# Head norm of the RWKV output moved from the output stage into the scan

## Chip, cores and metric

The kernel runs on one core of one Trainium2 chip. The metric is the device time of one execution in microseconds. Engines are named PE (matrix engine), DVE (vector), ACT (scalar), POOL (GpSimd) and SP (issues DMAs).

## What is computed

Two layers of a trunk over 2,048 tokens of width 1,024, all in float32. Each layer normalises x, projects it with one matrix of 3,972 columns, runs four mixers side by side (forgetting attention, RWKV-7, windowed attention, a short convolution), gates each with silu, projects back and adds x. The part that matters is the end of the RWKV-7 mixer, where y comes from a scan over tokens with 4 heads of 64 channels:

```python
mean = jnp.mean(y, axis=-1, keepdims=True)
var = jnp.mean((y - mean) ** 2, axis=-1, keepdims=True)
y = ((y - mean) * lax.rsqrt(var + RWKV_LN_EPS)).reshape(B, S, GROUP_W)
y = y * ln_g.astype(f32) + ln_b.astype(f32)
bonus = jnp.sum(r_h * k_h * r_k.astype(f32), axis=-1, keepdims=True) * v_h
y = y + bonus.reshape(B, S, GROUP_W)
```

## The kernel before

A layer is a series of stages with a barrier between them: `phase_project` (norm of x, turn to channels on the partitions, first columns of the projection), `phase_rwkv_prep` (what the scan needs, with projection matmuls between), `phase_rwkv_scan`, `phase_head_norm` (norms of the queries and keys of both attentions and the running sum of the forget gates), `phase_fox`, `phase_swa`, `phase_out`. Every projection matmul is split into three matmuls in a rounded format, high by high, low by high and high by low.

**The scan** (`phase_rwkv_scan`, names with `rs_`) handles 16 tiles of 128 tokens, two chunks of 64 each, in a loop of `Fori(0, NT // 2)` with two tiles in its body; ACT's loop has 7 turns and two tiles behind it, as its weight loads run ahead. Beside each tile goes one row tile of the projection: 96 matmuls of 512 columns ("fill", `J.pe_tile`, L124, L128, L130), cut by the table `SCAN_FILL` into portions that PE runs after each product of the scan, while DVE or ACT evacuates the product. The order on each engine is written out by hand and engines signal by semaphores. `units_done` says after which portion ACT evacuates an accumulator of the projection (every 24 matmuls).

The tile ends so: for both chunks c, PE accumulates 6 x 4 products with the state S (L740 to L744) and runs portion `c0` or `c1`; DVE scales the new S (L802), and with the second chunk signals `y_m`. ACT copies the half tiles of y from PSUM to `yt`, tokens on the partitions (L858). PE turns `yt` with two transposes (L749), so that channels lie on the partitions, and runs portion `y`; ACT copies the result to `yst` (L863) and frees the banks for the next tile (`y_ev`), whose transposes of inputs (L693) wait for that. SP stores `yst` to `mixT` in DRAM ahead of the last quarter of the projection row.

**The output stage** (`phase_out`, names with `ou_`) works in 4 blocks of 512 tokens, channels on the partitions. For a block, DVE forms the mix: `convolve` makes the short convolution, then the RWKV rows `y_[:, 2:4, :]` are normalised per head, then the gates (ACT's Tanh of `g`, L1647) are applied. The sums over the 64 channels of a head are matmuls with the block matrix `bones`: PE makes them for the mean (`head_sums`, L1692) and for the square (`head_squares`, L1699), and ACT makes the root by Ln and Exp (L1650, L1652). ACT then rounds the mix to `m_hi` (L1665), POOL takes `m_lo` (L1679), and PE multiplies with the output weights in 8 accumulations `d` of 24 matmuls (L1716 to L1720). `mix(1 - q, add_x)` for the next block runs beside the products of this one: `between(d)` is `add_x(d)`, DVE's addition of x to accumulator d (L1746). The first block's mix has nothing beside it. PE's head sums for the next block stand behind d = 0 and d = 2. ACT may round parts of the next mix only as PE releases them in d = 7 (`m_free`).

**Tables of ACT.** Ln, Exp and Tanh need a function table, and the compiler puts loads ahead of operations whose table isn't there. `phase_project` and `phase_fox` preload a set that has both Ln and Exp; the scan so far uses copies only.

## Time and profile before

| | |
|---|---|
| median of 3 runs | 3924.72 us (3920.46 to 3925.77) |
| the profiled execution, its own time | 3933.37 us |
| its span, first to last instruction | 3931.6 us |
| PE busy | 3370.1 us, 86% of the span |
| DVE busy | 1492.6 us, 38% |
| ACT busy | 994.4 us, 25% |
| POOL busy | 577.7 us, 15% |
| mean granted clock of PE | 0.895 of full |

The median comes from runs without a profile. The profiled execution is one more, so every duration and instant comes from that one. Matmul durations overlap in the records: the distance between starts says what one costs, not its length. A releaser "DVEq L610" or "ACTq" means that the engine's own queue stood at a wait.

### The profile page before, as it was taken

What the parts mean: (1) busy time and instruction counts of PE and PEld (TensorE: products, weight loads), DVE (VectorE), ACT (ScalarE), POOL (GpSimd) and SP (SyncE); (2) the same over time, 40 slices, a digit from 0 to 9 for tenths busy, and PEclk for the clock granted to TensorE, in tenths of its full rate; (3) what the DMA queues carried; (4) which work ended last, traced back from release to release, by engine and by line L of the source; (5) the groups of instructions that cost most, each with busy time, mean ns of one, the idle gap of its engine ahead of it and who ended that gap; (6) DMA issues with size and microseconds to landing.
All of it is one profiled execution on the core that took longest, in us unless ns stands there. A gap on an engine that the chain in (4) does not pass through costs nothing. (4 is left out here: it accounts for less than half of the span.)

```text
span 3931.6 us, 63187 instructions
## 1 busy us (share of the span) xinstructions
PE 3370.1 (86%) x24772; PEld 2388.4 (61%) x24772; DVE 1492.6 (38%) x1970; ACT 994.4 (25%) x1742; POOL 577.7 (15%) x328
## 2 busy tenths in 40 slices
PE   6979799999986889449889797999999887885399
PEld 4868677777752444337658686777777624443277
DVE  4137422222224555356331473122221245553553
ACT  4024321212231343222230242122111223332221
POOL 4101000000001122322140010000000002223311
PEclk9989899999995688769989898999999976887699
DMA  3235422222232100355321453222222231003452
GB/s 116 70 99 166 126 63 66 75 61 74 68 121 102 36 17 9 93 187 170 111 84 64 126 159 104 61 71 66 62 61 68 79 132 53 22 9 80 159 185 100
DMA packets 340705, 351.19 MB, mean 89 GB/s; under 512 B 94492, under 2 KB 245276, under 8 KB 336568
## 3 DMA queue, kind: packets, MB, share of 16 engines
q1 hardware_dynamic: 273864, 314.52, 24.9%
q10 hardware_dynamic: 66560, 32.54, 3.2%
q8 instruction: 224, 3.67, 0.4%
q14 instruction: 57, 0.47, 0.0%
HBM read 211.87 MB, written 135.10 MB: 88 GB/s over the span
## 5 line engine op out<-in xcount | busy, mean ns | idle before, releaser
L124 PE MATMUL rs_acc<-h_hi,rs_w_hi 128*128 128x512 f32 x1024 | 425.6, 416 | 0.0
L128 PE MATMUL rs_acc<-h_lo,rs_w_hi 128*128 128x512 f32 x1024 | 415.1, 405 | 0.0
L130 PE MATMUL rs_acc<-h_hi,rs_w_lo 128*128 128x512 f32 x1024 | 412.4, 403 | 0.0
L110 POOL TENSOR_TENSOR rs_w_lo<-rs_raw,rs_w_hi 128x1024 fp32r<-128x1024 f32 x32 | 76.2, 2381 | 1267.1 <-POOLq L109 1267.1
L1716 PE MATMUL ou_acc<-wo_hi,ou_m_hi 128*128 128x512 f32 x512 | 210.5, 411 | 57.4 <-PEq L1715 57.4
L124 PE MATMUL rp_acc<-h_hi,rp_w_hi 128*128 128x512 f32 x512 | 205.6, 401 | 40.6 <-PEq L121 40.6
L1358 ACT ACTIVATE fx_prob<-fx_ST 128x512 f32<-128x512 f32 (+3 forms) x320 | 157.3, 532 | 296.5 <-PE fx_ST L1228 158.7
L124 PEld LDWEIGHTS rs_acc<-h_hi,rs_w_hi 128*128 128x128 f32 x1024 | 192.1, 188 | 53.8 <-issue 16.5
L130 PEld LDWEIGHTS rs_acc<-h_hi,rs_w_lo 128*128 128x128 f32 x1024 | 192.3, 188 | 41.6
L141 ACT COPY rs_stage<-rs_acc 128x512 f32<-128x512 f32 x128 | 75.0, 586 | 562.3 <-ACTq L140 562.3
L128 PEld LDWEIGHTS rs_acc<-h_lo,rs_w_hi 128*128 128x128 f32 x1024 | 192.5, 188 | 35.8
L124 PE MATMUL pj_acc<-h_hi,pj_w_hi 128*128 128x512 f32 (+1 forms) x512 | 208.3, 407 | 5.3 <-PEq L121 5.3
L128 PE MATMUL rp_acc<-h_lo,rp_w_hi 128*128 128x512 f32 x512 | 207.8, 406 | 0.0
L130 PE MATMUL pj_acc<-h_hi,pj_w_lo 128*128 128x512 f32 (+1 forms) x512 | 205.7, 402 | 0.0
L128 PE MATMUL pj_acc<-h_lo,pj_w_hi 128*128 128x512 f32 (+1 forms) x512 | 205.2, 401 | 0.0
L1719 PE MATMUL ou_acc<-wo_hi,ou_m_lo 128*128 128x512 f32 x512 | 203.4, 397 | 0.0
L1720 PE MATMUL ou_acc<-wo_lo,ou_m_hi 128*128 128x512 f32 x512 | 203.3, 397 | 0.0
L130 PE MATMUL rp_acc<-h_hi,rp_w_lo 128*128 128x512 f32 x512 | 200.3, 391 | 0.0
L1182 PE MATMUL fx_O<-fx_prob,fx_vs 128*64 128x512 f32 (+3 forms) x640 | 183.6, 658 | 19.4 <-DVE fx_yo L1309 19.4
L1291 DVE TENSOR_REDUCE fx_nm<-fx_SS 128x2 f32<-128x1024 f32 (+3 forms) x160 | 163.4, 1061 | 62.3 <-PE fx_SS L1203 37.9
L1164 POOL TENSOR_TENSOR fx_sump<-fx_sump,fx_prob 128x1024 f32<-128x1024 f32 (+2 forms) x60 | 125.7, 2094 | 299.6 <-ACT fx_prob L1358 299.6
L1203 PE MATMUL fx_SS<-fx_kb,fx_qb 66*128 66x512 f32 (+3 forms) x320 | 126.9, 500 | 44.2 <-DVE fx_nm L1291 39.8
(262 smaller groups left out, 6105.2 us busy)
## 6 DMA issues: line engine op xcount, KB each, us to landing
projT<-rs_stage SPq DMA_DIRECT2D x128, 256.0 KB, 2.0
pj_xb<-x SPq DMA_DIRECT2D x32, 512.0 KB, 3.5
projT<-rp_stage SPq DMA_DIRECT2D x64, 256.0 KB, 3.1
rs_raw<-w_in ACTq DMA_DIRECT2D x32, 512.0 KB
rs_nat<-rw SPq DMA_DIRECT2D x128, 128.0 KB, 2.4
ou_g<-projT SPq DMA_DIRECT2D x32, 512.0 KB, 6.0
ou_stage<-x SPq DMA_DIRECT2D x64, 256.0 KB, 2.7
rp_pre<-projT SPq DMA_DIRECT2D x16, 899.5 KB, 7.7
```

Source lines behind the costliest of these rows:

```text
L110: self.nc.gpsimd.tensor_tensor(self.w_lo[q][:, :, 0:m], self.raw[:, :, 0:m], self.w_hi[q][:, :, 0:m].bitcast(F32), ALU.subtract).then_inc( ...
L124: ins = M(acc, self.w_hi[q][:, k, 0:m], self.h_hi[:, k, cols], start=(k == 0), stop=False)
L128: M(acc, self.w_hi[q][:, k, 0:m], self.h_lo[:, k, cols], start=False, stop=False)
L130: ins = M(acc, self.w_lo[q][:, k, 0:m], self.h_hi[:, k, cols], start=False, stop=(k == KC - 1))
L1164: G.tensor_tensor(sump[R % 2][:, :, lo:TB], sump[R % 2][:, :, lo:TB], prob[nt % NP][:, :, lo:TB], ALU.add).then_inc(s["add_p"], 1)
L1182: ins = M(O[64 * h:64 * h + 64, lo:TB], vs[p][:, j, 64 * h:64 * h + 64], prob[i % NP][:, h, lo:TB], start=(j == 0), stop=(j == keys[Q] - 1))
L1203: ins = M(SS[ns % 2][:, h, 0:w], Q2[p][h][0:HD + 2, t * 128:(t + 1) * 128], K2[p][h][0:HD + 2, c * TB:c * TB + w], start=True, stop=(c < Q))
L1291: V.tensor_reduce(nm[p][:, :, t, c:c + 1], SS[ns % 2][:, :, 0:width(t, c)], AX.X, ALU.max, negate=True).then_inc(s["m_rdy"], 1)
L1358: A(prob[nt % NP][:, h, lo:TB], ST[h][:, lo:TB], ACT.Exp).then_inc(s["p_rdy"], 1)
L1716: ins = M(a[:], m_hi[:, k, rows], wo_hi[:, k, cs], start=(k == 0), stop=False)
L1719: M(a[:], m_lo[:, k, rows], wo_hi[:, k, cs], start=False, stop=False)
L1720: ins = M(a[:], m_hi[:, k, rows], wo_lo[:, k, cs], start=False, stop=(k == KC - 1))
```

## The change

The scan now normalises y itself, on `yt`, where a token's 64 channels of a head lie in a row of memory: DVE takes the sum, subtracts the mean, squares, sums again and scales with the epsilon added; ACT makes Ln and Exp of 128x4 values; DVE multiplies, and PE's transposes read the product. The fill portion `c1`, between the last products and the transposes, becomes 20 matmuls instead of 10, portion `y` behind them 4 instead of 14. ACT preloads the table set with Ln and Exp at the stage's start. The output stage loses the sums by matmul, the root and their semaphores; the scale `ln_g`, the bonus `bv` and the offset `ln_b` stay there, in two `scalar_tensor_tensor` and one `tensor_tensor`, and the wait for y moves to just ahead of them. The accumulators of the sums and the load of `bones` go.

```diff
@@ -322,7 +322,7 @@
 
 PREP_FILL = (("th", 16), ("lora", 24), ("ssk", 20), ("bs", 36))
 
-SCAN_FILL = (("tok", 7), ("p2", 5), ("s3", 5), ("s4", 4), ("s5", 5), ("s6", 5), ("s7", 6), ("s8", 5), ("s9", 6), ("wz", 6), ("g", 8), ("c0", 10), ("c1", 10), ("y", 14))
+SCAN_FILL = (("tok", 7), ("p2", 5), ("s3", 5), ("s4", 4), ("s5", 5), ("s6", 5), ("s7", 6), ("s8", 5), ("s9", 6), ("wz", 6), ("g", 8), ("c0", 10), ("c1", 20), ("y", 4))
 assert sum(n for _, n in PREP_FILL) == sum(n for _, n in SCAN_FILL) == 3 * KC * NB
 
 
@@ -588,7 +588,8 @@
         p2, p4, p8, x1, xn, yy = (P.sb(n, [128, NH, 64]) for n in ("p2", "p4", "p8", "x1", "xn", "yy"))
         px, wz, p4t, gm = (P.sb(n, [128, NH, 2, 64]) for n in ("px", "wz", "p4t", "gm"))
         S = P.sb("S", [128, NH, 64])
-        yt = P.sb("yt", [128, NH * 64])
+        yt, yc, yq = P.sb("yt", [128, NH, 64]), x1, yy
+        ym, yv = P.sb("ym", [128, NH, 1]), P.sb("yv", [128, NH, 1])
         yst = P.sb("yst", [128, 2, 128])
         bk = P.ps("bk", [128, 6, 512])
         J = Projector(P, nc, l, w_in, h_hi, h_lo, projT)
@@ -600,7 +601,7 @@
             return bk[:, i, :].rearrange("p (h u t) -> p h u t", h=NH, u=2)
 
         sems = ("c_in", "n_rdy", "mb", "mk", "tok", "d_rdy", "p2_m", "p2t_m", "p2_a", "p2_d", "ak_rdy", "tok_ev", "s3a", "s3d", "p4_a", "x2_d", "s4a", "s4d", "p8_a", "x3_d",
-                "q_m", "q_a", "s5", "x4", "s6a", "s6d", "x4_a", "y_d", "s7", "x5", "s8a", "s8d", "x5_a", "y2_d", "s9", "x6", "wz_m", "wz_d", "g_m", "g_d", "s_m", "s_d", "s2_m", "s2_d", "y_m", "yt_a", "yt_m", "y_a", "y_ev", "y_st", "i_ok")
+                "q_m", "q_a", "s5", "x4", "s6a", "s6d", "x4_a", "y_d", "s7", "x5", "s8a", "s8d", "x5_a", "y2_d", "s9", "x6", "wz_m", "wz_d", "g_m", "g_d", "s_m", "s_d", "s2_m", "s2_d", "y_m", "yt_a", "yv_d", "yr_a", "yn_d", "yt_m", "y_a", "y_ev", "y_st", "i_ok")
         s = {n: P.sem(n) for n in sems}
         i_in, in_free = [P.sem(f"i_in{e}") for e in two], [P.sem(f"in_free{e}") for e in two]
         block = ctx.enter_context(nc.Block())
@@ -744,9 +745,9 @@
                             ins = M(o[u], gm[half[c], h, u, :], S[half[c], h, :], start=False, stop=True)
                     ins.then_inc(s[done], 1)
                     fill(f)
-                take(pe, s["yt_a"])
+                take(pe, s["yn_d"])
                 for p in two:
-                    ins = Tr(bk[:, 3, p * 128:(p + 1) * 128], yt[:, p * 128:(p + 1) * 128], ident[:])
+                    ins = Tr(bk[:, 3, p * 128:(p + 1) * 128], yq[:, 2 * p:2 * p + 2, :], ident[:])
                 ins.then_inc(s["yt_m"], 1)
                 fill("y")
             tiles(pe, body)
@@ -803,6 +804,20 @@
                     if c:
                         ins.then_inc(s["y_m"], 1)
                     v.drain().then_inc(s["s_d" if c == 0 else "s2_d"], 1)
+                take(v, s["yt_a"])
+                V.tensor_reduce(ym[:, :, 0], yt[:], AX.X, ALU.add)
+                v.drain()
+                V.scalar_tensor_tensor(yc[:], ym[:].to_broadcast([128, NH, 64]), -1.0 / HD, yt[:], ALU.mult, ALU.add)
+                v.drain()
+                V.tensor_tensor(yq[:], yc[:], yc[:], ALU.mult)
+                v.drain()
+                V.tensor_reduce(yv[:, :, 0], yq[:], AX.X, ALU.add)
+                v.drain()
+                V.tensor_scalar(yv[:], yv[:], 1.0 / HD, LN_EPS, ALU.mult, ALU.add)
+                v.drain().then_inc(s["yv_d"], 1)
+                take(v, s["yr_a"])
+                V.tensor_tensor(yq[:], yc[:], yv[:].to_broadcast([128, NH, 64]), ALU.mult)
+                v.drain().then_inc(s["yn_d"], 1)
             tiles(v, body)
 
         @block.scalar
@@ -811,7 +826,8 @@
             act.wait_ge(s["i_ok"], 2)
             act.sem_inc(s["y_st"], 16)
             act.sem_inc(s["y_ev"], 1)
-            C = nc.scalar.copy
+            C, A = nc.scalar.copy, nc.scalar.activation
+            nc.scalar.preload_act_table_set("natural_log_exp_and_others")
 
             def evac(stage):
                 for b in units_done(SCAN_FILL, stage):
@@ -855,8 +871,13 @@
                 evac("c0")
                 take(act, s["y_m"])
                 for c in two:
-                    C(yt[half[c], :], bk[half[c], 4 + c, 0:NH * 64])
+                    C(yt[half[c]], bk[half[c], 4 + c, 0:NH * 64].rearrange("p (h t) -> p h t", h=NH))
                 act.drain().then_inc(s["yt_a"], 1)
+                take(act, s["yv_d"])
+                A(yv[:], yv[:], ACT.Ln)
+                act.drain()
+                A(yv[:], yv[:], ACT.Exp, scale=-0.5)
+                act.drain().then_inc(s["yr_a"], 1)
                 evac("c1")
                 take(act, s["yt_m"])
                 take(act, s["y_st"], 16)
@@ -1561,18 +1582,17 @@
     with ExitStack() as ctx:
         P = Phase(nc, ctx, f"ou{l}")
         two = range(2)
-        pars, bones = P.sb("pars", [128, NPAR]), P.sb("bones", [128, 128])
+        pars = P.sb("pars", [128, NPAR])
         y = [P.sb(f"y{q}", [128, KC, TB]) for q in two]
         g = P.sb("g", [128, KC, TB])
         cv = [P.sb(f"cv{q}", [128, 3, 2, TB + 2]) for q in two]
         bv = [P.sb(f"bv{q}", [128, 2, TB]) for q in two]
-        th, sq = P.sb("th", [128, KC, TB]), P.sb("sq", [128, 2, TB])
+        th = P.sb("th", [128, KC, TB])
         m_hi, m_lo = P.sb("m_hi", [128, KC, TB], F32R), P.sb("m_lo", [128, KC, TB], F32R)
         stage = [P.sb(f"stage{q}", [128, TB]) for q in two]
-        pm, pv = P.ps("pm", [128, 2, TB]), P.ps("pv", [128, 2, TB])
         NA = 4
         acc = [P.ps(f"acc{q}", [128, TB]) for q in range(NA)]
-        names = ("c_in", "th_rdy", "u_rdy", "pm_rdy", "sq_rdy", "pv_rdy", "v_rdy", "r_rdy", "mix_rdy", "hi_rdy", "lo_rdy", "m_free", "g_in", "g_free")
+        names = ("c_in", "th_rdy", "mix_rdy", "hi_rdy", "lo_rdy", "m_free", "g_in", "g_free")
         s = {n: P.sem(n) for n in names}
         acc_rdy, acc_free = ([P.sem(f"{n}{q}") for q in range(NA)] for n in ("acc_rdy", "acc_free"))
         cv_in, y_in, y_free, stage_in, stage_rdy, stage_st = (
@@ -1591,7 +1611,6 @@
         @block.sync
         def _(sp):
             sp.dma_start(pars[:], lay(par, l)).then_inc(s["c_in"], 16)
-            sp.dma_start(bones[:], consts[:, 256:384]).then_inc(s["c_in"], 16)
 
             def load_block(i, q):
                 cols = bass.ds(i * TB, TB)
@@ -1645,11 +1664,6 @@
                 act.wait_ge(s["g_in"], 64)
                 act.sem_inc(s["g_in"], -64)
                 A(th[:], g[:], ACT.Tanh, scale=0.5).then_inc(s["th_rdy"], 1)
-                act.wait_ge(s["v_rdy"], 1)
-                act.sem_inc(s["v_rdy"], -1)
-                A(sq[:], sq[:], ACT.Ln)
-                act.drain()
-                A(sq[:], sq[:], ACT.Exp, scale=-0.5).then_inc(s["r_rdy"], 1)
 
             act.sem_inc(s["g_free"], 1)
             gates()
@@ -1683,24 +1697,6 @@
         @block.tensor
         def _(pe):
             M = nc.tensor.matmul
-            pe.wait_ge(s["c_in"], 32)
-
-            def head_sums(q):
-                pe.wait_ge(s["u_rdy"], 1)
-                pe.sem_inc(s["u_rdy"], -1)
-                for p in two:
-                    ins = M(pm[:, p, :], bones[:], y[q][:, 2 + p, :], start=True, stop=True)
-                ins.then_inc(s["pm_rdy"], 1)
-
-            def head_squares():
-                pe.wait_ge(s["sq_rdy"], 1)
-                pe.sem_inc(s["sq_rdy"], -1)
-                for p in two:
-                    ins = M(pv[:, p, :], bones[:], sq[:, p, :], start=True, stop=True)
-                ins.then_inc(s["pv_rdy"], 1)
-
-            head_sums(0)
-            head_squares()
             pe.sem_inc(s["m_free"], KC // 2 - 1)
 
             def body(i, q, follows, load):
@@ -1721,16 +1717,12 @@
                         if d == KC - 1 and k % 2 == 1 and k < KC - 1:
                             ins.then_inc(s["m_free"], 1)
                     ins.then_inc(acc_rdy[d % NA], 1)
-                    if d == 0 and follows:
-                        head_sums(1 - q)
-                    if d == 2 and follows:
-                        head_squares()
             blocks(pe, body)
 
         @block.vector
         def _(v):
             V = nc.vector
-            v.wait_ge(s["c_in"], 32)
+            v.wait_ge(s["c_in"], 16)
             for q in two:
                 v.sem_inc(stage_st[q], 16)
             for q in range(NA):
@@ -1760,42 +1752,25 @@
                     for p in two:
                         V.scalar_tensor_tensor(y_[:, 6 + p, :], cv_[:, 1, p, w:TB + w], pars[:, C_CW + 2 * w + p:C_CW + 2 * w + p + 1], y_[:, 6 + p, :], ALU.mult, ALU.add)
 
-            def mix(q, between, first=False):
+            def mix(q, between):
                 y_, g_, cv_ = y[q], g, cv[q]
-                if first:
-                    convolve(q)
-                v.wait_ge(y_in[q], 32)
-                v.sem_inc(y_in[q], -32)
-                v.drain().then_inc(s["u_rdy"], 1)
-                if not first:
-                    convolve(q)
-
-                v.wait_ge(s["pm_rdy"], 1)
-                v.sem_inc(s["pm_rdy"], -1)
-                V.scalar_tensor_tensor(y_[:, 2:4, :], pm[:], -1.0 / HD, y_[:, 2:4, :], ALU.mult, ALU.add)
+                convolve(q)
                 v.drain()
-                V.tensor_tensor(sq[:], y_[:, 2:4, :], y_[:, 2:4, :], ALU.mult).then_inc(s["sq_rdy"], 1)
                 between(0)
                 V.tensor_tensor(y_[:, 6:8, :], y_[:, 6:8, :], cv_[:, 0, :, 2:TB + 2], ALU.mult)
                 between(1)
-                v.wait_ge(s["pv_rdy"], 1)
-                v.sem_inc(s["pv_rdy"], -1)
-                V.tensor_scalar(sq[:], pv[:], 1.0 / HD, LN_EPS, ALU.mult, ALU.add).then_inc(s["v_rdy"], 1)
-                between(2)
-
                 v.wait_ge(s["th_rdy"], 1)
                 v.sem_inc(s["th_rdy"], -1)
                 V.scalar_tensor_tensor(g_[:, 0:4, :], th[:, 0:4, :], 1.0, g_[:, 0:4, :], ALU.add, ALU.mult)
+                between(2)
                 V.scalar_tensor_tensor(g_[:, 4:8, :], th[:, 4:8, :], 1.0, g_[:, 4:8, :], ALU.add, ALU.mult)
                 between(3)
-                v.wait_ge(s["r_rdy"], 1)
-                v.sem_inc(s["r_rdy"], -1)
-                V.tensor_tensor(y_[:, 2:4, :], y_[:, 2:4, :], sq[:], ALU.mult)
+                v.wait_ge(y_in[q], 32)
+                v.sem_inc(y_in[q], -32)
+                for p in two:
+                    V.scalar_tensor_tensor(y_[:, 2 + p, :], y_[:, 2 + p, :], pars[:, C_LG + p:C_LG + p + 1], bv[q][:, p, :], ALU.mult, ALU.add)
                 v.drain()
-                for p in two:
-                    V.tensor_scalar(y_[:, 2 + p, :], y_[:, 2 + p, :], pars[:, C_LG + p:C_LG + p + 1], pars[:, C_LB + p:C_LB + p + 1], ALU.mult, ALU.add)
-                v.drain()
-                V.tensor_tensor(y_[:, 2:4, :], y_[:, 2:4, :], bv[q][:], ALU.add)
+                V.tensor_tensor(y_[:, 2:4, :], y_[:, 2:4, :], pars[:, C_LB:C_LB + 2].rearrange("p (k o) -> p k o", o=1).to_broadcast([128, 2, TB]), ALU.add)
                 between(4)
                 v.drain()
                 V.scalar_tensor_tensor(y_[:, 0:4, :], g_[:, 0:4, :], 0.5, y_[:, 0:4, :], ALU.mult, ALU.mult)
@@ -1804,7 +1779,7 @@
                 between(6)
                 between(7)
 
-            mix(0, lambda d: None, first=True)
+            mix(0, lambda d: None)
 
             def body(i, q, follows, load):
                 if follows:
```

## Rows read from the trace of the kernel before

**Rows 1.** Scan stage, layer 0: us, busy PE PEld DVE ACT POOL, clock, DMA share, GB/s.
```profile
458.00:1138.00 680.00, 663.18 (x8089) 518.35 (x8090) 146.36 (x293) 136.35 (x319) 38.10 (x16) 0.98 0.24 67
```

**Rows 2.** Timeline (start us, length, engine, line), scan, end of a tile.
```profile
595.86 0.50 PE L124 MATMUL rs_acc<-h_hi,rs_w_hi 128*128 128x512 f32 x1
...
596.18 0.42 DVE L802 TENSOR_TENSOR rs_S<-rs_bk,rs_pend 64x256 f32<-64x256 f32 x1 [3.60 <-DVEq L610]
596.19 0.39 PE L128 MATMUL rs_acc<-h_lo,rs_w_hi 128*128 128x512 f32 x1
...
596.72 0.74 ACT L858 COPY rs_yt<-rs_bk 64x256 f32<-64x256 f32 x2 [1.55 <-ACTq L610]
...
598.03 0.39 PE L124 MATMUL rs_acc<-h_hi,rs_w_hi 128*128 128x512 f32 x1
...
598.26 0.38 PE L749 MATMUL rs_bk<-rs_ident,rs_yt 128*128 128x128 f32 x2
...
598.85 0.38 ACT L863 COPY rs_yst<-rs_bk 128x256 f32<-128x256 f32 x1 [1.39 <-ACTq L610]
...
604.14 1.09 PE L693 MATMUL rs_bk<-rs_ident,rs_nat 128*128 128x128 f32 x8
```

**Rows 3.** Groups by line and shape: busy, mean ns, idle before.
```profile
L774 DVE TENSOR_TENSOR rs_px<-rs_br,rs_eye 64x256 f32<-64x256 f32 x64 | 26.9, 420 | 3.6
...
L1291 DVE TENSOR_REDUCE fx_nm<-fx_SS 128x2 f32<-128x256 f32 x16 | 6.7, 419 | 1.4 <-PE fx_SS L1205 1.1
...
L233 ACT ACTIVATE pj_rst<-pj_rst 128x1 f32<-128x1 f32 x32 | 6.5, 203 | 2.2
```

**Rows 4.** Timeline of the window attention: small operations and handovers.
```profile
1657.22 0.20 DVE L1529 RECIPROCAL sw_ls<-sw_ls 128x8 f32<-128x8 f32 x1
1657.53 1.90 POOL L1425 TENSOR_TENSOR sw_pr<-sw_pr,sw_ls 128x1024 f32<-128x1024 f32 x1 [5.31 <-DVEq L1530]
```

**Rows 5.** Timeline of the output stage, layer 0, from blocks 0 and 1.
```profile
1749.54 1.88 PE L1692 MATMUL ou_pm<-ou_y,ou_bones 128*128 128x512 f32 x4
...
1751.49 0.40 PE L1719 MATMUL ou_acc<-wo_hi,ou_m_lo 128*128 128x512 f32 x1
...
1782.58 2.29 DVE L1803 SCALAR_TENSOR_TENSOR ou_y<-ou_g,ou_y 128x2048 f32<-128x2048 f32 x1
...
1788.26 1.06 ACT L1665 ACTIVATE ou_m_hi<-ou_y 128x1024 fp32r<-128x1024 f32 x1 [17.67 <-ACTq L1664]
```

**Rows 6.** Timeline of the output stage's opening, layer 0, then layer 1.
```profile
1723.23 2.29 DVE L1788 SCALAR_TENSOR_TENSOR ou_g<-ou_th,ou_g 128x2048 f32<-128x2048 f32 x1 [0.20 <-DVEq L1787]
...
3701.25 3.62 ACT L1647 ACTIVATE ou_th<-ou_g 128x4096 f32<-128x4096 f32 x1
...
3706.24 2.28 DVE L1788 SCALAR_TENSOR_TENSOR ou_g<-ou_th,ou_g 128x2048 f32<-128x2048 f32 x1
...
3711.33 1.23 DVE L1793 TENSOR_TENSOR ou_y<-ou_y,ou_sq 128x1024 f32<-128x1024 f32 x1 [0.61 <-DVEq L1792]
3712.64 1.00 DVE L1796 TENSOR_SCALAR ou_y<-ou_y,ou_pars 128x512 f32<-128x512 f32 x2
...
3715.01 2.29 DVE L1801 SCALAR_TENSOR_TENSOR ou_y<-ou_g,ou_y 128x2048 f32<-128x2048 f32 x1
```

**Rows 7.** Timeline of the head-norm stage, layer 0.
```profile
1157.50 1.28 ACT L937 ACT_TABLE_LOAD   x1
...
1162.61 0.12 PEld L957 LDWEIGHTS hn_bk<-hn_sq,hn_gather 128*14 128x14 f32 x2 [1.64 <-issue]
...
1184.54 1.28 ACT L945 ACT_TABLE_LOAD   x1
```

**Rows 8.** Groups by line: table loads of the scalar engine.
```profile
L514 ACT ACT_TABLE_LOAD x16 | 20.5, 1283 | 3.8 <-ACTq L513 3.7
...
L497 ACT ACT_TABLE_LOAD x4 | 5.1, 1283 | 9.3 <-ACTq L496 9.3
...
L1647 ACT ACT_TABLE_LOAD x2 | 2.6, 1283 | 46.7 <-ACTq L1646 46.7
```

## The prediction

> **What bounds the kernel now.** I read the page's busy table first, then each stage by its own stretch, then timelines around the code that changes. The matrix engine PE sets the pace. In the scan it is busy 663 of 680 us at a granted clock of 0.98 of full speed, while the vector engine DVE and the scalar engine ACT work 146 and 136 us [rows 1]. The reader is to see that PE's order is fixed by hand: small products of the scan, and between them matmuls of the projection ("fill") that cover what DVE and ACT do. A scan product waits for an answer only if its fill is too short. So an operation on DVE or ACT costs nothing until it outlasts the fill behind which it stands. At the end of a tile, fill starts at 595.86, one matmul each 0.23 us (598.03 less 596.19, over 8), and the two transposes of y follow the tenth at 598.26, without a gap; ACT had finished `yt` at 596.72 + 0.74 = 597.46 [rows 2]. Nobody waits there now.
>
> The output stage is bound by PE too, but here the norm uses PE itself: four fp32 matmuls with `bones` take the place of one moment twice in each block that prepares a follower. In the opening of this stage no fill exists, and the chain ACT, DVE sets the time to PE's first product.
>
> **Scan, added chain.** Per tile, DVE gets five operations, then ACT two, then DVE one, and PE waits for the last. Durations: the reduction over 128x256 is 419 ns and a two-input operation of 256 elements a row 420 ns, a tiny ACT operation 203 ns [rows 3]; a tiny DVE operation 0.20, and from its end to another engine's start 0.11 us [rows 4]. Between two dependent DVE operations with a drain lie 0.08 us (3711.33 + 1.23 to 3712.64) [rows 6]. From DVE's S at 596.18 + 0.42 to ACT's copy lie 0.12 [rows 2]; I take 0.12 for each crossing.
> - crossing ACT to DVE 0.12
> - sum, subtract, square, sum, scale: 4 x 0.42 + 0.20 + 4 x 0.08 = 2.20
> - crossing 0.12; Ln, drain, Exp 0.20 + 0.08 + 0.20 = 0.48
> - crossing 0.12, multiply 0.42, crossing 0.12: 0.66
> The sum is 3.58, from 597.46 to 601.04. PE, now with 20 fill matmuls, would come to the transposes at 598.26 + 10 x 0.23 = 600.56. So it waits 0.48 us per tile, in 16 tiles of two layers: **+15.4 us**. The fill that moves from behind the transposes to ahead of them is the same work; without it the wait would be 2.8.
>
> Bounds. Below: without gaps and with half the crossings the chain is 3.58 - 0.40 - 0.24 = 2.94, which is hidden, so 0. Above: from the end of the transposes (598.26 + 0.38) to ACT's copy lie 0.21 [rows 2]; four crossings of that length add 0.36, a restart of PE after the wait perhaps 0.1 (an estimate from one crossing), so 0.94 per tile, 30 us. I keep the middle because each term has a row of nearly its own kind; the weakest are the two reductions out of SBUF.
>
> Other queues of the scan. Behind ACT's new wait stand the copy `yst` and the last evacuation. The copy frees PE for the next tile's transposes at 604.14 and ended at 599.23 [rows 2]; with transposes 2.8 later it ends near 602, and the next tile is late by 0.48 as well. About 2.5 us remain, so nothing more. SP takes `y_a` before the last projection store; its issue moves by the same, and the store has a whole tile before it is missed. The final store of a layer comes after four fill matmuls still, so the end of the stage moves only by its waits. DVE has nothing to do until the next tile's first product. The table preload, 1.28 us once per layer [rows 8], lies in the opening wait for inputs, ahead of the first fill; if not, 2.6 in all. `x1` and `yy` are reused between their last reader of a tile and their first writer of the next: no wait.
>
> On drains the row and a page part. After a 1.23 us DVE operation the next starts 0.08 later [rows 6]. The Trainium skill ("VectorE: DVE Perf Modes", The DRAIN you can't avoid) has a gap of the operation's duration less 266 ns after each. By it each gap here would be about 154 ns, the wait 0.78, and the change of the kernel -4.6 instead of -14.2 us; the row at hand speaks against adding it on top of the duration.
>
> **Output stage, removed.** In each block with a follower PE loses two groups of four matmuls. The first begins at 1749.54, where the next product would stand; that product's second matmul starts at 1751.49 instead of 1749.54 + 0.23 [rows 5]: 1.72 us. Two groups, 3 blocks, 2 layers: 12 x 1.72 = **-20.6 us**. This holds only if DVE still delivers in time. It ended the mix at 1782.58 + 2.29 = 1784.87 and ACT's copy, released by PE in the last eighth, came at 1788.26 [rows 5], so 3.4 us to spare. The mix's last part still follows the same accumulator (`between(5)`), thus both ends move together. POOL's splitting, which gaps PE at the start of a block, is untouched. The gate load is released by `mix_rdy` as before, and ACT now has only Tanh there.
>
> Opening, layer 0: DVE's first gate operation already waited for Tanh (idle 0.20 ahead of 1723.23) [rows 6], so its start stays. Then go the wait for the root and the stretch from L1793 to L1801, 3715.01 - 3711.33 = 3.68. In its place come two operations of 512 elements and one of 1,024: I price them by proportion at 0.72, 0.72 and 1.23 with two gaps, 2.8. That gives 0.88 and the wait. The wait is 0.61 in layer 1 [rows 6]; in layer 0 it is 0.3 (ACT's chain has the same parts). In layer 1 Tanh ended at 3701.25 + 3.62 = 3704.87, but DVE started at 3706.24 for the sake of the second moment: 1.2 more. Together 1.2 + 2.7 = **-3.9 us**. The dropped load of `bones` is taken as nothing; one short issue on SP, it can only help.
>
> **Head-norm stage, moved by the tables.** Today ACT comes there with the table of the preparation and loads a table between Exp and Ln (1157.50) and again ahead of the last Exp (1184.54), 1.28 each [rows 7]. With the combined set preloaded in the scan both can go. The second stands alone on the path: -1.28. Behind the first, the third tile's square is late and PE's loading idles 1.64 ahead of 1162.61 [rows 7], more than the load, and the stretch after it is PE's: -1.28. In two layers **-5.1 us**; below, 0 if the loads stay.
>
> **Sum.** +15.4 - 20.6 - 3.9 - 5.1 = -14.2. The profiled execution took 3933.4 by its own time (span 3931.6), 8.7 above the median of 3924.7; in its own scale the result is 3919.2, in that of the median 3910.5. I say 3911.
>
> **Rivals.**
> 1. *The wait is hidden* (crossings and gaps shorter). Then -29.6: 3895. For it: the 0.48 is the small difference of 3.58 and 3.10. Against it: every term has a close row. 15%.
> 2. *The chain is longer,* 0.94 a tile: 30.1 - 29.6, no change: 3925. Crossings through a drain may each add. 12%.
> 3. *A table load in every loop turn.* If the state of the table isn't carried over the loop's head, Ln gets a load after its wait. The preparation loads 4 times at L497, twice in each layer, that is once per turn of its loop, though it left the turn before with a fitting table [rows 8]; that loop was entered with another table, this one would not be. In the scan 14 turns x 1.28 = 17.9 on the chain: 3928. 8%. The Trainium skill ("ScalarE activation tables: per-element evaluation and per-set limits", Table sets in the compiler and the runtime) says that loads are placed per block by greedy longest run, which is this case. Of the trace, the loop of the preparation fits that rule, but L1647 does not: it loads once a layer [rows 8], though its loop and the blocks behind it use Tanh again.
> 4. *The other side: two loads in each tile.* L514 has a load in all 16 units, for Ln right between Exps [rows 8]. If the preload doesn't hold in the loop, Ln and Exp of each tile load, 2 x 1.28 x 32 = 82 us on the chain: 3993. It decides from 0.93 us of waiting per tile (29.6 / 32). Against it: the initial norm and the attention preload the same set and show no load between their Ln and Exp. 7%.
> 5. *The change doesn't save in the output stage* because DVE or a load becomes late there: against it the 3.4 us to spare. 3%; 3931.
> My forecast itself has 55%.
>
> **Range and chances.** A measurement of this kernel tells about 0.2%, 8 us, from no change. The forecast's own range, by the bounds of the wait it calls likely (0.2 to 0.8 a tile), is 3901 to 3921. To hold eight in ten I take in the hidden case and most of the longer ones: 3895 to 3929. Faster by over 0.2%: 15% and 85% of the 55%, 0.62. Slower: case 4, a part of 3 and 5 and a chain beyond the bound, 0.14. The rest, 0.24, within.
>
> **What the profile will show.** In the scan, an idle of about half a us ahead of L749's successor in each tile and no table load in the loop; period of a tile 0.5 longer. In the output stage blocks with a follower 3.4 us shorter, PE's first product 1.2 and 2.7 us sooner after the stage's start. In the head norm no table load and 2.6 us less. I am wrong if a load shows in the scan, if the wait is nearer 0 or 1, or if PE in the output stage idles at a block's start for more than before.

## The result and the profile after

The changed kernel takes 3970.17 us (median of 4, 3968.9 to 3978.56), the kernel before 3922.59 on the same chip (3909.63 to 3925.77): ratio 1.0136, 95% interval 1.0111 to 1.0162. It is slower by about 48 us where 14 us less were forecast, and above the range. The profiled execution after took 3970.19 (span 3968.4), so it lies on its median, while that of before (3933.37) lay 8.7 above the 3924.72 of its own three runs; the two spans differ by 36.8.

Stage by stage, from the first DMA of each stage to that of the next (of the input projection from its second, 0.4 later; the last stage to the end of the span), in us:

| stage | before, layer 0 / 1 | after, layer 0 / 1 | difference |
|---|---|---|---|
| input projection | 234.6 / 235.9 | 233.9 / 234.8 | -1.8 |
| preparation | 222.6 / 222.9 | 224.1 / 222.7 | +1.3 |
| scan | 685.7 / 724.7 | 727.9 / 752.0 | **+69.5** |
| head norm | 113.6 / 111.8 | 109.7 / 110.7 | -5.0 |
| full attention | 334.2 / 330.9 | 337.8 / 324.0 | -3.3 |
| window attention | 106.8 / 106.1 | 106.8 / 106.8 | +0.7 |
| output | 250.0 / 250.7 | 238.4 / 237.7 | **-24.6** |

Output stage and head norm gave what was forecast (24.5 and 5.1). The scan took 69.5 more where 15.4 were allowed. The windows view of the kernel after, for the stretch of [rows 1], for the whole scan of layer 0 and for that of layer 1:

```profile
458.00:1138.00 680.00, 638.11 (x7581) 495.75 (x7582) 171.70 (x364) 135.32 (x328) 38.14 (x16) 0.97 0.23 65
458.00:1186.30 728.30, 682.16 (x8096) 529.23 (x8096) 183.47 (x389) 144.71 (x353) 38.14 (x16) 0.97 0.22 63
2420.00:3172.00 752.00, 686.83 (x8019) 530.62 (x8018) 184.59 (x389) 147.59 (x353) 38.14 (x16) 0.96 0.22 63
```

PE was busy 663 of 680 us; now it is 638, and 7581 matmuls came in the time in which 8089 did [rows 1]. So time is lost between matmuls. The view of waits for PE names where, first in the scan of layer 0, then of layer 1 (total us, times, longest):

```profile
PE rs_bk L668 <- PEq L611: 38.9, 8, 20.8
PE rs_bk L750 <- PEq L611: 6.7, 16, 0.4
...
PE rs_bk L668 <- PEq L611: 39.6, 8, 20.7
PE rs_bk L668 <- issue: 19.3, 7, 3.6
PE rs_bk L750 <- PEq L611: 6.7, 16, 0.4
```

L750 is the forecast wait for the norm, 16 times 0.42 us of idle. L668 is the first group of products of a tile: one wait of 20.8 is the opening of the stage, and seven more make 18.1 us in layer 0. In layer 1 another seven, of up to 3.6 us, stand at "issue": there PE waited for nothing that the profile shows. Seven is the number of turns of the scan's loop (eight turns of two tiles, seven between them). The distance from one copy of `yt` to the next shows it as well. Before, all 15 distances of layer 0 are 41.38 to 41.43. After, every tile inside a turn takes 42.20 to 42.22 and every one across a turn 46.22 to 46.64. In layer 1 the kernel before already had this: 41.4 inside, 44.3 to 48.1 across; after, it is 42.2 and 47.9 to 51.4. I had read the scan of layer 0 alone.

The account of the scan: 0.82 in each of 16 tiles is 13.1 a layer. The seven turns of layer 0 lose 29.9 more (4.3 each); those of layer 1 lose 53.5 where they lost 39.1. Together 26.2 + 29.9 + 14.4 = 70.5, against 69.5 measured.

The timeline after, at the end of the second tile of layer 0, for what [rows 2] show of before:

```profile
556.18 0.75 ACT L874 COPY rs_yt<-rs_bk 64x256 f32<-64x256 f32 x2 [1.55 <-ACTq L611]
...
557.09 0.42 DVE L808 TENSOR_REDUCE rs_ym<-rs_yt 128x4 f32<-128x256 f32 x1 [1.03 <-DVEq L611]
...
557.59 0.42 DVE L810 SCALAR_TENSOR_TENSOR rs_x<-rs_ym,rs_yt 128x256 f32<-128x256 f32 x1
...
559.10 0.17 DVE L816 TENSOR_SCALAR rs_yv<-rs_yv 128x4 f32<-128x4 f32 x1
...
559.42 0.20 ACT L877 ACTIVATE rs_yv<-rs_yv 128x4 f32<-128x4 f32 x1 [2.50 <-ACTq L611]
...
559.70 0.21 ACT L879 ACTIVATE rs_yv<-rs_yv 128x4 f32<-128x4 f32 x1
559.85 0.40 PE L128 MATMUL rs_acc<-h_lo,rs_w_hi 128*128 128x512 f32 x1
560.07 0.43 DVE L819 TENSOR_TENSOR rs_yy<-rs_x,rs_yv 128x256 f32<-128x256 f32 x1 [0.81 <-DVEq L611]
560.67 0.41 PE L750 MATMUL rs_bk<-rs_ident,rs_yy 128*128 128x128 f32 x2 [0.42 <-PEq L611]
...
561.62 0.40 PE L130 MATMUL rs_acc<-h_hi,rs_w_lo 128*128 128x512 f32 x1
564.84 1.12 PE L668 MATMUL rs_bk<-rs_bt,rs_cr 64*64 64x64 f32 x16 [2.82 <-PEq L611]
565.71 1.94 PE L668 MATMUL rs_bk<-rs_cr,rs_bt 64*64 64x128 f32 x16
```

The norm's chain is there as forecast. What is new stands in the last three lines: after the fourth fill matmul PE does nothing for 2.82 us, and then its products run slowly. Inside a turn the same sixteen products take 0.68 us and follow the fill at once. The kernel before, at the same turn and then at the first one of layer 1:

```profile
555.29 0.74 ACT L858 COPY rs_yt<-rs_bk 64x256 f32<-64x256 f32 x2 [1.55 <-ACTq L610]
...
556.84 0.38 PE L749 MATMUL rs_bk<-rs_ident,rs_yt 128*128 128x128 f32 x2
...
560.03 0.39 PE L130 MATMUL rs_acc<-h_hi,rs_w_lo 128*128 128x512 f32 x1
560.38 0.68 PE L667 MATMUL rs_bk<-rs_bt,rs_cr 64*64 64x64 f32 x16
...
2505.80 0.38 PE L749 MATMUL rs_bk<-rs_ident,rs_yt 128*128 128x128 f32 x2
2510.42 0.41 PE L667 MATMUL rs_bk<-rs_bt,rs_cr 64*64 64x64 f32 x6 [1.04 <-PEq L610]
2513.26 0.80 PE L667 MATMUL rs_bk<-rs_bt,rs_cr 64*64 64x64 f32 x10 [2.43 <-issue]
```

**The time of a turn.** PE's last wait of a turn is released when the operation before it ends. Before, that is ACT's copy of `yt` (started 555.29, 0.74 long, so 556.03), and the next turn's first product runs at 560.38 without a gap: 4.35 us or less were needed, all of it under queued work. After, it is DVE's L819, which ends at 560.50, and the product runs at 564.84: 4.34 us, with fill only until 562.0. At the fourteen turns of the changed kernel it is 3.8 to 4.4 us, inside a turn 1.45. In layer 1 of the kernel before a second stall falls inside a group of sixteen products, where nothing in the program waits; that fits a PE that had been given no instructions. The queue that moves instructions agrees. The DMA view (packets, MB, share) of 0.2 us of the kernel after at 561.7 has one packet:

```profile
q8 instruction: 1, 0.02, 43.6%
```

That of before has one in 0.2 us at 557.4 and one in 0.3 us at 2510.8:

```profile
q8 instruction: 1, 0.02, 40.5%
...
q8 instruction: 1, 0.02, 18.7%
```

At the two turns of layer 0 the packet runs 1.3 and 1.5 us after the release and 3.1 and 2.9 us ahead of the turn's first product; in layer 1 the packet at 2510.9 runs 2.3 us ahead of the end of the stall inside the group. All seven turns of layer 0 have such a packet: it starts 2.1 to 2.3 us after the start of the copy of `yt` in the kernel before and 5.6 to 6.0 us after it in the kernel after, where the release comes 3.6 us later; inside a turn none starts in the 8 us behind that copy. The Trainium skill ("Runtime: NRT & Kernel Launch", Instruction fetch mechanics) says that instructions are streamed in blocks of 16 KiB, that the cost of a new block is mostly hidden, and that a taken branch to a block that isn't held stalls until it has been fetched. The size agrees (3.67 MB in 224 packets before), and so does the stall at a turn; the page gives it no duration, here it is hidden only while PE has about 4.3 us of queued work. My prediction did not weigh this rule.

**The clock.** The windows of 562.0 to 564.8 and of 564.8 to 568.5, after:

```profile
562.00:564.80 2.80, 0.01 (x1) 0.00 (x0) 0.00 (x0) 0.59 (x1) 0.00 (x0) 0.98 0.44 126
564.80:568.50 3.70, 3.67 (x46) 3.69 (x48) 1.65 (x2) 0.00 (x0) 0.00 (x0) 0.56 0.88 216
```

Behind the idle the granted clock is 0.56, near the level of 1.2 GHz, and 1.00 again from 568.5. The loss is 2.82 + 3.7 x 0.44 = 4.4 us, which is about the 4.3 of a turn.

**What else the profile after shows.** Groups of ACT's table loads, and the opening of the output stage in layer 0 and layer 1:

```profile
L830 ACT ACT_TABLE_LOAD x2 | 2.6, 1283 | 21.2 <-DVEq L766 21.2
...
L1666 ACT ACT_TABLE_LOAD x2 | 2.6, 1283 | 46.1 <-ACTq L1665 46.1
```
```profile
1765.65 2.29 DVE L1764 SCALAR_TENSOR_TENSOR ou_g<-ou_th,ou_g 128x2048 f32<-128x2048 f32 x1 [10.55 <-DVEq L1763]
...
1781.40 0.77 PE L1712 MATMUL ou_acc<-wo_hi,ou_m_hi 128*128 128x512 f32 x1 [44.68 <-PEq L1711]
...
3770.43 0.76 PE L1712 MATMUL ou_acc<-wo_hi,ou_m_hi 128*128 128x512 f32 x1 [44.35 <-PEq L1711]
```

The preload is one load a layer and stands in the opening wait. There is none in the scan's loop and none in the head norm, where [rows 7] had two. PE's first product of the output stage comes 40.0 and 39.7 us after the stage's first DMA, where it was 41.6 and 42.6; from there to the end it is 198.3 and 198.0 where it was 208.4 and 208.1.

### The profile page after: what moved, and what is told of

Same layout as the page of the kernel before. It is cut to its first block and busy times, and to the rows that moved or that the text cites. A ratio compares the mean times of both kernels' runs of the same rounds, so it can differ in the third digit from the quotient of the medians.

```text
span 3968.4 us, 63527 instructions
## 1 busy us (share of the span) xinstructions
PE 3360.1 (85%) x24708; PEld 2385.2 (60%) x24708; DVE 1535.2 (39%) x2130; ACT 967.6 (24%) x1772; POOL 578.9 (15%) x328
## 5 line engine op out<-in xcount | busy, mean ns | idle before, releaser
L1712 PEld LDWEIGHTS ou_acc<-wo_hi,ou_m_hi 128*128 128x128 f32 x512 | 97.1, 190 | 141.4 <-issue 118.5
```

What stands on the lines that cost most here:

```text
L1712: ins = M(a[:], m_hi[:, k, rows], wo_hi[:, k, cs], start=(k == 0), stop=False)
```

## Experiments

All ratios are against the kernel before, run beside each group on the same chip; its median was 3927.07 beside experiments 1 to 4, 3917.86 beside 5 to 8 and 3915.17 beside 9 to 12. So medians of different groups are compared by their ratios, and stages by the profiled executions.

**1. The moved fill alone.** The kernel before, with the changed kernel's table.
```diff
-... ("c0", 10), ("c1", 10), ("y", 14))
+... ("c0", 10), ("c1", 20), ("y", 4))
```


> The kernel before with the fill table of the kernel after (c1 20, y 4) and nothing else. Three theories on the 2.8 us for which PE idles at each turn of the scan's loop in layer 0. Turn theory (deep): PE's queue needs some 4.2 us from the moment when it passes its last wait to have the instructions of the next turn; here yt is ready early, the queue is not held, it runs ahead behind 20 fill matmuls and the stall stays hidden: time as before, 3922, tile periods 41.4 in layer 0 without exception. Turn theory (shallow): PE's queue gets no further ahead than the few matmuls behind the transposes, so the four fill matmuls alone cause it: layer 0 has turns of about 45.5, +40 to +47 us in all. Data theory: something of the next tile (inputs, freed banks) is late because it hangs on the added norm chain: no stall here, 3922.


Measured: 3927.08, ratio 0.9998 (0.9983 to 1.0013); the tiles of layer 0 stay at 41.38 to 41.51. With four fill matmuls behind the transposes there is no stall in layer 0, as long as the wait is released early. So there it is not the fill's place but the time of the release. The turns of layer 1 take 45.3 to 49.0 with the same early release, as slow as in the kernel before (44.3 to 48.1); experiments 8 to 10 go into that.

**2. The norm with the old fill.** The changed kernel with `("c1", 10), ("y", 14)`.


> The kernel after with the fill table of the kernel before (c1 10, y 14). Norm chain of 3.7 us less 1.3 us of fill: each tile waits about 2.9 us, period near 44.2. Turn theory (both forms): behind the wait stand 14 fill matmuls, 3.2 us and the transposes 0.3, so the turn is hidden but for 0.6 us: turns at most 0.6 to 1 longer than the other tiles in layer 0; total 3970 - 30 (layer 0 turns) - about 14 (layer 1 turns) + 2.4 x 32 = near 4003. Data theory: the stall at the turn stays at about 4.4, total near 4040.


Measured: 4000.41, ratio 1.0177 (1.0146 to 1.0208). The timeline at the turn:
```profile
563.52 0.41 PE L750 MATMUL rs_bk<-rs_ident,rs_yy 128*128 128x128 f32 x2 [2.75 <-PEq L611]
...
566.80 0.40 PE L130 MATMUL rs_acc<-h_hi,rs_w_lo 128*128 128x512 f32 x1
567.68 0.68 PE L668 MATMUL rs_bk<-rs_bt,rs_cr 64*64 64x64 f32 x16 [0.48 <-PEq L611]
```
The wait is the 2.8 of the prediction, in each tile. But from the transposes to the first product are 4.16 us, as they are 4.17 in the changed kernel; fourteen matmuls cover all but 0.48 of it here, all but 0.42 at one other turn of layer 0, and all of it at the other five. At this turn the time after the release is the same, with cover for it or without. The total came out as expected, the tiles did not: they take 44.5 to 47.3 where 44.2 was expected. The rest is mostly the granted clock, which fell to half at ten of the sixteen waits of layer 0, as behind the third:
```profile
608.60 0.41 PE L750 MATMUL rs_bk<-rs_ident,rs_yy 128*128 128x128 f32 x2 [2.75 <-PEq L611]
...
609.40:612.90 3.50, 3.50 (x10) 2.73 (x9) 0.00 (x0) 0.19 (x1) 0.00 (x0) 0.51 0.13 37
```

**3. The turns taken out: PE's tiles written out.** The other engines keep their loops.
```diff
-            tiles(pe, body)
+            for t in range(NT):
+                body(t, None, t % 2)
```


> The kernel after with PE's loop over the tiles written out (16 tiles in a row on PE alone, the other engines loop as before). Turn theory: all tiles take 42.2, in layer 0 7 x 4.3 = 30 us go and in layer 1 7 x 7.6 = 53 us: near 3887. Data theory: nothing changes, 3970.


Measured: 3888.67, ratio 0.9901 (0.9872 to 0.993); scans of 698.0 and 698.6; all tiles 42.21 in both layers.
```profile
560.72 0.41 PE L750 MATMUL rs_bk<-rs_ident,rs_yy 128*128 128x128 f32 x2 [0.42 <-PEq L611]
...
561.67 0.40 PE L130 MATMUL rs_acc<-h_hi,rs_w_lo 128*128 128x512 f32 x1
562.00 0.68 PE L668 MATMUL rs_bk<-rs_bt,rs_cr 64*64 64x64 f32 x16
```
The wait for the norm is the same 0.42, and the stall of 2.82 behind it is gone with the turn. By the medians this one edit takes 81 us off the changed kernel. No instruction packet starts between 553.4 and 567.8 us, the stretch around the transposes; the whole kernel has 192 of them where the changed one has 218.

**4. The same edit in the kernel before.**


> The kernel before with PE's loop over the tiles written out. Turn theory: layer 0 has no stall and stays, layer 1 has turns of 44.3 to 48.1 against 41.4 and loses 7 x 5.6 = 39 us: near 3883. Data theory: 3922. With e3 the difference of the two is then the change without its loop effect, about +0.8 x 32 - 30 = -4 us.


Measured: 3888.66, ratio 0.9891 (0.9858 to 0.9924); all tiles 41.39, scans of 685.9 and 685.5. Its gain is all in layer 1. Beside experiment 3 this prices the change without turns: nothing that the intervals can tell. The norm costs 12.1 and 13.1 us in the two scans, and the output stage gives that back.

**5. The turns out and the norm covered.** Experiment 3 with `("c0", 6), ("c1", 24)`.


> The kernel after, PE's tile loop written out, and four fill matmuls moved from portion c0 to c1 (c0 6, c1 24, y 4). The added cover of 0.93 us is more than the 0.8 us that a tile is longer than before. Norm-wait theory: the transposes are reached after yn_d, every tile falls from 42.21 back to 41.4, 32 x 0.8 = 26 us: 3888 - 26 = 3862. Rival: 6 matmuls are too few behind the first half's products, or the later copy yst holds the next tile: the period stays at 42.2 or rises, 3888 or more.


Measured: 3870.45, ratio 0.9887 (0.9859 to 0.9914); tiles of 41.58, scans of 687.7 and 687.5. Against the kernel before it is 47 us less where the expectation had 65. By the ratios the step from experiment 3 (0.9901) is inside the noise; that the norm's wait is covered is read from the scans of the profiled executions, together 21 us shorter than there, where 26 were expected.
```profile
557.58 0.39 PE L128 MATMUL rs_acc<-h_lo,rs_w_hi 128*128 128x512 f32 x1
...
557.81 0.38 PE L750 MATMUL rs_bk<-rs_ident,rs_yy 128*128 128x128 f32 x2
```
PE no longer waits. Of the 0.82 us of a tile 0.63 was the wait, 0.19 stays though no idle time is shown.

**6. The loop kept, four more matmuls behind the wait.** The changed kernel with `("c0", 6), ("c1", 20), ("y", 8)`.


> The kernel after with its loop, four fill matmuls moved from c0 to the portion behind the transposes (c0 6, c1 20, y 8). From the traces so far PE's first product of a turn starts 4.17 us after the release of the last wait. Turn theory: the idle at the turn in layer 0 falls from 2.8 by 4 x 0.233 to about 1.9, with its slow products the turn's tile from 46.5 to 45.3; other tiles stay at 42.2; in both layers 14 x 1.2 = 16 us: 3954. If the stall were a fixed price of the loop, nothing changes: 3970.


Measured: 3933.94 (five executions, 3928.22 to 3952.14), ratio 1.006 (1.0031 to 1.0088); turns of layer 0 at 44.0 to 46.3. The profile is of the execution of 3928.22.
```profile
564.81 0.68 PE L668 MATMUL rs_bk<-rs_bt,rs_cr 64*64 64x64 f32 x16 [2.13 <-PEq L611]
565.30 1.07 PE L668 MATMUL rs_bk<-rs_cr,rs_bt 64*64 64x128 f32 x16
```
The stall shrinks by 0.7, four matmuls being 0.9, and at this turn the products keep their speed. It is 16 us above the kernel before where 31 were expected. In the profiled execution five of the seven turns of layer 0 lose no clock, which is part of the difference. The time from the release to the first product is 3.8 to 4.9 us here, so it is not quite the same at every turn.

**7. Without the table preload.** The call of `preload_act_table_set` is left out.


> The kernel after without the preload of the table set in the scan. What the forecast's rival had: two loads per tile, 2 x 1.28 us on the norm chain in 32 tiles, 82 us, and the two loads of the head-norm stage back, 5 us: near 4057. If the compiler places one load per loop turn only: near 3970 + 18 + 5 = 3993.


Measured: 4070.39 (one run). The groups by line:
```profile
L876 ACT ACT_TABLE_LOAD x32 | 41.1, 1283 | 79.3 <-ACTq L611 79.3
L878 ACT ACT_TABLE_LOAD x32 | 41.1, 1283 | 1.8
```
Two loads a tile, all on the chain, and the scans take 783.9 and 791.5, 95.5 us more than in the changed kernel. The loads themselves are 82 of it, as rival 4 had it; behind the longer wait the clock falls too (0.79 in the 3.5 us from 570.5), which rival 4 left out. It was a true mechanism that the preload keeps away.

**8. The output stage alone.** The changed kernel's output stage behind the scan and fill of before; the head norm is computed nowhere.


> The output stage of the kernel after with the scan and fill table of the kernel before: no head norm is computed anywhere, so the output is that of a kernel without it. By the forecast's terms -20.6 and -3.9 us, the head-norm stage unchanged: 3927 - 25 = 3902. Rival: part of the 49 us that the rest of the kernel after won back came from elsewhere, then less than 20 here.


Measured: 3871.59, ratio 0.9882 (0.9857 to 0.9906): 46 us below the kernel before where 25 were expected. The output stages are 238.0 and 238.9, scan of layer 0 685.8 as before. But the scan of layer 1, the same code as before, takes 692.1 in place of 724.7, its turns 41.9 to 42.9 in place of 44.3 to 48.1:
```profile
2483.95 0.39 PE L130 MATMUL rs_acc<-h_hi,rs_w_lo 128*128 128x512 f32 x1
2484.27 0.68 PE L667 MATMUL rs_bk<-rs_bt,rs_cr 64*64 64x64 f32 x16
...
2487.36 0.59 PE L667 MATMUL rs_bk<-rs_cr,rs_kt 64*64 64x128 f32 x6 [0.88 <-issue]
```
For layer 1's loop in PE's program only one thing is new: the output stage ahead of it is shorter, so the loop stands elsewhere. In the profiled executions the output stages give 24 us and this scan 33.

**9 and 10. The place of the loop alone.** The kernel before, with semaphore instructions that nobody waits for ahead of layer 1's scan, 64 and 160 of them.
```diff
+            if l == 1:
+                for _ in range(32):
+                    pe.sem_inc(s["pad"], 1)
+                    pe.sem_inc(s["pad"], -1)
```


> The kernel before with 64 semaphore instructions that nothing waits for put in TensorE's program just ahead of the second layer's scan. Placement theory (the cost of the loop's turn depends on where the loop stands in TensorE's program): layer 0 stays at 41.4 us a tile, and the tiles at a turn in layer 1 move away from their mean of 47 us, to anything from 41.9 to 48. Rival (the second layer's turns are slow for its data or its transfers): they stay near 47 us and the time near 3920 us.

> The same with 160 such instructions. Placement theory: another mean of the turns of layer 1 than without them or with 64. Rival: near 47 us again, the time near 3920 us.


Measured: 3885.59 with 64, ratio 0.9907 (0.9884 to 0.9931), and 3906.32 with 160, ratio 0.9967 (0.9942 to 0.9993). In both the turns of layer 1 fall to 41.38 to 41.72. With 64 the timeline at the turn has no gap:
```profile
2504.78 0.38 PE L753 MATMUL rs_bk<-rs_ident,rs_yt 128*128 128x128 f32 x2
...
2507.97 0.39 PE L130 MATMUL rs_acc<-h_hi,rs_w_lo 128*128 128x512 f32 x1
2508.29 0.68 PE L671 MATMUL rs_bk<-rs_bt,rs_cr 64*64 64x64 f32 x16
```
64 instructions that do nothing make the kernel before 30 us faster: its scan of layer 1 takes 685.3. With 160 the tiles are as short, but the stage's opening grows (PE's idle there is 36.2 against 21.7 us) and the scan is 701.0. The rival, data or transfers of layer 1, falls.

**11. Four tiles in a turn.** The changed kernel with three turns inside a layer's scan in place of seven.
```diff
-            tiles(pe, body)
+            with pe.Fori(0, NT // 4) as i:
+                for u in range(4):
+                    body(None, None, u % 2)
```


> The changed kernel with four tiles in TensorE's loop body in place of two, so three turns inside a layer's scan in place of seven. Turn theory: tiles of 42.2 us except at three places in each layer, so layer 0's scan loses 4 x 4.3 = 17 us of its 727.9 and layer 1's about 30 of its 752; about 3925 us. Rival (the turn costs nothing by itself, the stall comes with every second tile for its buffers): the stalls stay at every second tile, near 3970 us.


Measured: 3925.36, ratio 1.0018 (0.9998 to 1.0037); every fourth distance is 47.4 to 47.6 in layer 0 and 50.8 to 51.5 in layer 1, all others 42.2. The stall goes with the turn, not with the pair of buffers. A turn costs 5.3 here, a little more than 4.3.

**12. The best of both.** Experiment 3 with `("c0", 6), ("c1", 22), ("y", 6)`.


> The changed kernel with TensorE's tiles written out, 22 fill matmuls ahead of the transposes and 6 behind. Turn theory with the wait for the norm covered: tiles of 41.4 to 41.6 us in both layers, no wait of TensorE at the transposes, 3862 to 3872 us, 0.986 to 0.989 of before.


Measured: 3864.89, ratio 0.9855 (0.9835 to 0.9876); tiles of 41.73 to 41.74, scans of 690.0 and 690.2, output stages of 238.5 and 237.8. It beats both kernels, and its interval lies below that of experiment 9 beside it, the kernel before without its bad turns, by 21 us in the medians. It overlaps those of experiments 4 and 5, and the scans of 5 are shorter, so that this is the best division of the fill isn't shown. The stages say what the change is worth once turns and wait are out of the way: the scans cost 8.7 us more than in experiment 9, the output stages 24.4 less than before, the head norm about 3 less, together some 18 us. The kernel before was not run with its turns out and this table.

## Why the prediction was wrong

The step that failed stands in the first part: an operation on DVE or ACT "costs nothing until it outlasts the fill behind which it stands", and in the second: the fill moved from behind the transposes to ahead of them "is the same work". It is the same work inside a turn. Across a turn the fill behind the last wait is what PE works on until the next turn's first product can run, 3.8 to 4.4 us after the release by the traces. Before, the release came at 556.03 and the queued work lasted until 560.38. After, it comes at 560.50 and the work until 562.0, so 2.8 us are bare, and the clock falls behind them. The runs showed this from four sides: without the turns the stall is gone (3), with fewer turns it comes less often (11), with more fill behind the wait it shrinks (6, 2), and with the moved fill alone it doesn't come in layer 0 (1). That the missing thing is the supply of instructions is argued from the packets and from the stall inside a group; the dependence on the loop's place alone (8, 9, 10) supports it. What about the place makes the turns of layer 1 slow although the release comes early there is not shown. No rival of mine had the turn as its place, though layer 1 of the kernel before lost 39 us at its turns; I had not looked at it.

The gap, in spans: forecast -14.2, measured +36.8, so 51.0. The turns are 44.3 of it (29.9 and 14.4), the wait in each tile 10.8 (32 times 0.82 - 0.48), stages that the change doesn't touch and roundings -4.1. To the median of 3970 come the 8.7 by which the profiled execution of before was long: the forecast took them off, the execution after had no such excess.

Term by term:
- **The wait for the norm,** forecast 0.48: right in kind, too small. The chain took 3.74 where 3.58 was worked out, since each of four crossings is 0.16, not 0.12; five operations on DVE took 2.18 for 2.20. The wait was 0.59 by the start of the transposes (560.67 instead of 560.08, one matmul of 0.23 behind the last), 0.63 by experiment 5. Another 0.19 a tile stays unexplained. With 0.82 in place of 0.48 the forecast would still have said faster by 3.
- **The drain:** between two dependent operations of DVE lie 0.08 us (557.51 to 557.59), as the row of the output stage said. By the rule of the Trainium skill ("VectorE: DVE Perf Modes", The DRAIN you can't avoid) it would be 0.15 (an estimate, 0.42 less 0.266); the trace disagrees.
- **Output stage,** -20.6 in the blocks: -10.0 and -10.1, right. **Opening,** -1.2 and -2.7: -1.6 and -2.9.
- **Head norm,** -5.1: -5.0 in these two executions, but some of that is chance. The stage is 111.5 us in the mean over the seven kernels that have the two loads (110.4 to 113.6) and 110.1 over the seven that have not (109.2 to 112.8), so about 2.8 in two layers.
- **Rivals 3 and 4,** table loads: none in the loop. Of the rule cited there, that loads are placed per block (the Trainium skill, "ScalarE activation tables: per-element evaluation and per-set limits", Table sets in the compiler and the runtime), nothing shows once the set is preloaded; without it, the kernel behaves as rival 4 says, and is 95.5 us slower in the scans instead of 82. **Rivals 1, 2 and 5:** the wait isn't hidden, its chain is inside the bound of 0.94, the output stage saves.

## What to carry to other kernels

Ahead of a loop's turn look at how much queued work an engine has behind its last wait. In PE's loop here about 4.3 us were needed: a later release there cost the stall and often the clock behind it, even where the work was only reordered. That is measured on this one loop, and in layer 1 of the kernel before 4.4 us of work were not enough. Read the distance between the same instruction of successive turns, in every layer, before pricing an edit; two alternating distances, as in layer 1 here, are a sign that the turn is already bare. Where a kernel changes by tens of us and its stages don't say why, write the tightest engine's loop out, or shift it by a few dead instructions, before judging the edit itself.

## What the runs showed of the hardware

- A turn of PE's loop: where PE is idle there, the first product runs 4.34 us after the release of the last wait at the turn shown, and 3.8 to 4.4 us over the fourteen turns of the changed kernel (experiment 2 has 4.16 from the transposes, the changed kernel 4.17). The Trainium skill ("Advanced Engine Details and Errata", Control Flow Timing) has some 0.1 us for a compare and branch; no run here shows that time by itself.
- The same loop, with the same data, loses 39 us at its turns or next to nothing, depending on 64 instructions ahead of it (724.7 or 685.3 us).
- The granted clock fell to 0.56 behind 2.82 us of idle at a turn, which came after 0.42 idle and only six matmuls. Behind the 2.75 us of idle that each tile of experiment 2 has, between long runs of matmuls, both levels are seen: it stayed at 1.00 behind the second wait (563.5 to 567.2) and was 0.51 behind the third (609.4 to 612.9). Why is not shown.
- 160 semaphore instructions in a row lengthened a stage's opening by 14.6 us against 64 of them.
